# Attention values of two steps made together in every odd step, from three buffers of turned probabilities

## The chip, the cores and the metric

The kernel runs on one core of a Trainium2 chip. The metric is the device time of one execution in microseconds (us); lower is better. The kernel before takes 1966.2 us (median of 3 runs, 1966.16 to 1966.59).

## The reference

The program is a decoder trunk of two layers over 1024 tokens and 1024 columns. The first layer mixes tokens by pooling, the second by attention; each layer also has a SwiGLU block and an update gated by an embedding. The change lies in the attention of the second layer: 16 query heads share 4 key/value heads (4 queries to one), each of 64 columns, and each block of 128 queries sees its own 128 keys and the 128 before.

```
scores = q . k * HEAD_DIM ** -0.5          # a block of 128 queries against 256 keys
scores = where(valid, scores, NEG_INF)     # causal, window of 128
probs  = softmax(concat([scores, sink]))[..., :-1]
out    = probs . v                         # 128 queries x 64 columns for each head
m      = out @ w_o
h      = h + rms_norm(m, mix_post_g)
```

## The kernel before

Attention is worked off in 32 steps. Step n holds one block of 128 queries (t = n // 4) and one key/value head (g = n % 4) with its four query heads. Every engine runs its own list of instructions in order, written out by hand; the lists are tied by semaphores. For step n there are these pieces, named by one letter in the prediction where they are TensorE's:

- S(n), `scores`, L1635: four products of queries and keys on TensorE, into one of two pairs of banks (n odd or even). Before S(n) writes its pair, TensorE waits until the exponentials of step n-2, which read the same pair, are done (`at_probs`).
- `softmax_max`, L1646 and L1651, on VectorE: mask and row maximum of four heads, then the gap to the sink.
- `softmax_exp`, L1660 and L1663, on ScalarE: one small and four large exponentials, from the bank into `probs`, each with its row sum.
- `softmax_recip`, L1671 and L1673, on VectorE, and `softmax_norm`, L1681, on GpSimd: the probabilities are divided by their sums.
- T(n), `turn_probs`, L1689: eight 128x128 transposes on TensorE into banks 4 and 5. It waits for the normed probabilities and until bank 4 and bank 5 of step n-1 have been copied out.
- `probs_copy_even` (VectorE, L1696, bank 4) and `probs_copy_odd` (ScalarE, L1702, bank 5): the turned probabilities are copied to one of two buffers, `pt[n % 2]` (the trace names them tmp and pt). The copy waits for the values of step n-2.
- V(n), `values`, L1716: four products with the values on TensorE, each with 64 output columns, into bank 6 or 7. They wait for both copies of step n and for the output copy of step n-2.
- `att_out`, L1726, on ScalarE: the outputs of step n are copied from the bank to `qo`.

The order of the lists in step n of the loop over 32 steps is:

- TensorE: T(n), S(n+4), V(n-1)
- ScalarE: exponentials of n+2, output copy of n-2, bank 5 copy of n
- VectorE: reciprocal of n+1, maximum of n+3, bank 4 copy of n
- GpSimd: norm of n; behind step 16 and step 18 also the two halves of the first output block (L1753, L1757)

In the last steps TensorE's list holds the first two of the eight blocks of the output projection too (`o_pe_first`, L315 to L317), between S and T of step 31, with pieces of their weights cut on ScalarE (L287) and VectorE (L291). Ahead of the attention ScalarE waits until the query weights are cut, and then issues the load of the row of gains of the next block (`gain_row("ffn1", ...)`, L604). Behind the attention it waits for V(31), issues the load of another row (`post_gain`, L604 too) and cuts the five remaining weight blocks of the output projection; the projection's third block and those behind it wait for these.

Of the kernel before, what the change touches and what calls it, by code (L numbers as in the profile page):

```python
# [22 lines left out]
P = 128  # L23
F32 = mybir.dt.float32
# [3 lines left out]
ACT = mybir.ActivationFunctionType  # L28
AX = mybir.AxisListType

D = 1024
# [3 lines left out]
KD = D // P  # L35
HALF = 512
# [54 lines left out]
def trunk(nc, I, out):  # L91
    ctx = ExitStack()
    with ctx:
# [36 lines left out]
        def region(name, elements, *uses):  # L130

            views = {}
            for use in uses:
                with ExitStack() as inner:
                    for n, shape, dt in use:
                        views[n] = inner.enter_context(nc.sbuf_tensor(n, shape, dt))
            sb(name, [P, elements])
            return views
# [17 lines left out]

        PIECES = [P, 4, 4, P]
        FORM = [P, 4, P]
        GAIN_VIEWS = region("gain_or_late_activations", D, [("gain", [P, D], F32)], [("act_late", [P, 2, HALF], F32)])
        gain, ACT_LATE = GAIN_VIEWS["gain"], GAIN_VIEWS["act_late"]  # L160
        Z = region("Z", 186 * KIB,

# [57 lines left out]
        xn, tmp = [Z["xn0"], Z["xn1"]], Z["tmp"]  # L220
# [19 lines left out]
        ps = ctx.enter_context(nc.psum_tensor("ps", [P, 8, HALF], F32))  # L240
# [17 lines left out]
        BASE, n = {}, 0  # L258
# [7 lines left out]
        w_ready = sem("weights_ready")  # L266
# [335 lines left out]
        def row_load(eng, dst, src, s):  # L602

            eng.dma_start(dst[:, :], src.partition_broadcast(P)).then_inc(s, 16)  # L604
# [66 lines left out]
        m7, up0_last, act_late = Z["m7"], Z["up0_last"], ACT_LATE  # L671
# [942 lines left out]

        STEPS_A = TILES * KV_HEADS
        probs = [DD[f"probs{g}"] for g in range(KV_HEADS)]
        pt = [tmp[:, :].rearrange("p (k c) -> p k c", k=KD), E["pt1"]]
        mask = B["mask"]
        neg_sinks_set = sem("neg_sinks_set")
        at_scores, at_neg_max, at_gap = [sem(f"att_{x}") for x in ("scores", "neg_max", "sink_gap")]  # L1620
# [70 lines left out]

        def probs_copy_even(dve, n):
            dve.wait_ge(at_turned, n + 1)
            if n >= 2:
                dve.wait_ge(at_pv, n - 1)
            dve.tensor_copy(pt[n % 2][:, 0:4, :].rearrange("p a b -> p (a b)"), ps[:, 4, :]).then_inc(at_pt_even, 1)  # L1696

        def probs_copy_odd(act, n):
            act.wait_ge(at_turned, n + 1)
            if n >= 2:  # L1700
                act.wait_ge(at_pv, n - 1)
            act.activation(pt[n % 2][:, 4:8, :].rearrange("p a b -> p (a b)"), ps[:, 5, :], ACT.Copy).then_inc(at_pt_odd, 1)  # L1702

        def values(pe, n):

            t, g = n // 4, n % 4
            pe.wait_ge(at_pt_even, n + 1)
            pe.wait_ge(at_pt_odd, n + 1)
            if n == 0:
                pe.wait_ge(q_copied, 1 + TILES)  # L1710
            if n >= 2:
                pe.wait_ge(at_out, n - 1)
            by_block = pt[n % 2].rearrange("p (m b) c -> p m b c", b=2)
            for b in range(2):
                for r in range(2):
                    last = pe.matmul(ps[HEAD * r:HEAD * (r + 1), 6 + g % 2, (g // 2) * 256:(g // 2 + 1) * 256  # L1716
                                        ].rearrange("p (m c) -> p m c", m=2),
                                     V[:, t + b, g * HEAD:(g + 1) * HEAD], by_block[:, 2 * r:2 * r + 2, b, :],
                                     start=(b == 0), stop=(b == 1))
            last.then_inc(at_pv, 1)  # L1720

        def att_out(act, n):

            t, g = n // 4, n % 4
            act.wait_ge(at_pv, n + 1)
            act.activation(qo[:, t, g * 256:(g + 1) * 256], ps[:, 6 + g % 2, (g // 2) * 256:(g // 2 + 1) * 256], ACT.Copy  # L1726
                           ).then_inc(at_out, 1)
# [282 lines left out]
        def _(act):  # L2010
            def gain_row(name, src):
                row_load(act, gain, src, gain_loaded)
# [125 lines left out]


            staggered(act, q_parts, before=kv_parts, head=False, tail=False)  # L2140
            act.wait_ge(w_ready, BASE["q"] + KD)
            gain_row("ffn1", I["ffn_pre_g"][1])

            def o_cut_hi(k):
                cut_hi(act, BASE["o"], k, w_o[0][:, k, :])
# [7 lines left out]
            for n in range(STEPS_A):  # L2153
                if n + 2 < STEPS_A:
                    softmax_exp(act, n + 2)
                if n == STEPS_A - 1:
                    o_cut_hi(EARLY)
                if n >= 2:
                    att_out(act, n - 2)
                probs_copy_odd(act, n)  # L2160
            for n in range(STEPS_A - 2, STEPS_A):
                att_out(act, n)

            def o_cuts(i, p):
# [3 lines left out]
            def o_gain(i, p):  # L2168
                act.wait_ge(at_pv, STEPS_A)
                row_load(act, post_gain, I["mix_post_g"][1], post_gain_loaded)  # L2170

            staggered(act, [(0, at_first(o_gain)), (0, at_first(o_cuts)), (1, not_first(lambda i, p: o_hi(act, i, p))),
                            (-2, lambda i, p: fn_raw(act, 1, i, p)), (-1, lambda i, p: fn_squares(act, 1, i, p)),
# [184 lines left out]
        @block.tensor  # L2358
        def _(pe):
            pe.wait_ge(first_consts_loaded, 16)  # L2360


            def pool_products(i, p):
                s = s_pool
                pe.wait_ge(s["lo"][p], s.done("lo", i))
                pe.wait_ge(s["added"][p], s.free("added", i))
                pe.wait_ge(pool_w_ready, 2)
                for g in range(len(WINDOWS)):
                    for k in range(2):
                        last = product(pe, banks(2 + 2 * p)[:, g * GROUP:(g + 1) * GROUP],  # L2370
                                       [x[p][:, 2 * g + k, :] for x in (xt_hi, xt_lo)],
                                       [x[:, 2 * g + k, :] for x in w_pool], k == 0, k == 1)
                last.then_inc(s["used"][p], 1)

            staggered(pe, [(1, lambda i, p: pool_band(pe, i, p)), (0, at_last(pool_products)),
                           (-2, lambda i, p: fn_turn(pe, 0, i, p)), (0, not_last(pool_products))],
                      tail=False, unrolled=True)

            def ffn(L):
                last = GROUPS - 1  # L2380
                ffn_pe_first(pe, L)
                ffn_pe_tile(pe, L, 0, 1)
                with pe.Fori(1, last) as g:
                    for t in range(2):
                        ffn_pe_tile(pe, L, g, t)
                for t in range(2):
                    ffn_pe_tile(pe, L, last, t)
                ffn_pe_down(pe, L, last, 0, (last, 1))
                ffn_pe_down(pe, L, last, 1, (last, 1),
                            lambda name, j: turn(pe, S[f"ple{L}"], 0, 0) if (name, j) == ("S1", 1) else None)  # L2390
                keep_busy(pe, 10, 2)
                pe.wait_ge(F["summed"], SUMMED * (half_of(L, GROUPS, 0) + 1))

            def turned(s):
                return lambda i, p: turn(pe, s, i, p)

            ffn(0)
            ple_parts = [[(0, lambda i, p, L=L: ple_pe(pe, L, i, p))] for L in range(2)]
            kv_parts = [(1, turned(s_kv)), (0, lambda i, p: kv_pe(pe, i, p)), (-1, lambda i, p: kv_turn(pe, i, p))]
            def first_scores(i, p):  # L2400
                pe.wait_ge(s_kv["lo"][1], s_kv.done("lo", PAIRS - 1))
                scores(pe, 0)

            q_parts = [(0, at_last(first_scores)), (0, lambda i, p: q_pe(pe, i, p, [0])),
                       (-1, lambda i, p: q_turn(pe, i, p)), (0, at_last(lambda i, p: scores(pe, 1))),
                       (0, lambda i, p: q_pe(pe, i, p, [1]))]
            staggered(pe, ple_parts[0], after=kv_parts, head=False, unrolled=True)
            pe.wait_ge(w_ready, BASE["kv"] + 4)
            staggered(pe, kv_parts, after=q_parts, head=False, tail=False)
            staggered(pe, q_parts, before=kv_parts, head=False, tail=False)  # L2410


            pe.wait_ge(v_copied, TILES)
            scores(pe, 2)
            q_turn(pe, PAIRS - 1, 1)
            scores(pe, 3)
            for n in range(STEPS_A):
                if n == STEPS_A - 1:
                    o_pe_first(pe, range(EARLY))
                turn_probs(pe, n)  # L2420
                if n + 4 < STEPS_A:
                    scores(pe, n + 4)
                if n >= 1:
                    values(pe, n - 1)
            values(pe, STEPS_A - 1)


            staggered(pe, [(0, lambda i, p: o_pe(pe, i, p))], head=False, tail=False, unrolled=True)
            ffn(1)
            staggered(pe, ple_parts[1], head=False, unrolled=True)  # L2430
# [26 lines left out]
```

## Time and profile before

| | |
|---|---|
| runs, median (lowest to highest) | 1966.2 us (1966.16 to 1966.59) |
| the profiled execution | 1965.92 us |
| its span, first to last instruction | 1964.1 us |
| mean granted TensorE clock | 0.998 of full |
| TensorE busy, matmul | 1917.4 us (98%) |
| VectorE busy | 1402.6 us (71%) |
| ScalarE busy | 905.4 us (46%) |
| GpSimd busy | 457.5 us (23%) |
| T of step 0 starts, last V starts | 1000.6 us, 1100.7 us |

Busy time is the union of an engine's instructions; matmuls are pipelined, so that a busy TensorE is not one at its peak. The attention steps are some 5% of the span, and only they are changed. A row of the timeline gives the start, how long the group lasted, the engine, the line, what is written and read, how many instructions the group has, and in brackets how long the engine was idle ahead of it and who ended that. The weight loads of TensorE have the name PEld, instructions that only its or another engine's queue handles a q (ACTq). The engines of the trace are PE (TensorE), DVE (VectorE), ACT (ScalarE) and POOL (GpSimd).

### The profile page before, as it was taken

What the parts mean: (1) busy time and instruction counts of PE and PEld (TensorE: products, weight loads), DVE (VectorE), ACT (ScalarE), POOL (GpSimd) and SP (SyncE); (2) the same over time, 40 slices, a digit from 0 to 9 for tenths busy, and PEclk for the clock granted to TensorE, in tenths of its full rate; (3) what the DMA queues carried; (4) which work ended last, traced back from release to release, by engine and by line L of the source; (5) the groups of instructions that cost most, each with busy time, mean ns of one, the idle gap of its engine ahead of it and who ended that gap; (6) DMA issues with size and microseconds to landing.
All of it is one profiled execution on the core that took longest, in us unless ns stands there. A gap on an engine that the chain in (4) does not pass through costs nothing.

```text
span 1964.1 us, 28703 instructions
## 1 busy us (share of the span) xinstructions
PE 1917.4 (98%) x9198; PEld 1573.6 (80%) x9198; DVE 1402.6 (71%) x2382; ACT 905.4 (46%) x1734; POOL 457.5 (23%) x448
## 2 busy tenths in 40 slices
PE   7899999999999999999999999999999999999998
PEld 7778888888888878888866787788888888888787
DVE  5987777777777786565389658777777777777863
ACT  6744444444444453341178545444444444444531
POOL 2312222222222221010046211212122221222310
PEclk9999999999999999999999999999999999999999
DMA  5333332233333350254200213233333223335201
GB/s 201 108 97 104 91 91 87 76 102 91 107 91 91 92 200 22 78 219 172 86 12 2 66 42 123 71 107 92 98 94 91 86 75 106 91 106 176 99 30 67
DMA packets 222055, 188.50 MB, mean 96 GB/s; under 512 B 12192, under 2 KB 199968, under 8 KB 221984
## 3 DMA queue, kind: packets, MB, share of 16 engines
q1 hardware_dynamic: 217712, 183.38, 29.2%
q10 hardware_dynamic: 4272, 4.21, 0.7%
q8 instruction: 40, 0.66, 0.1%
q14 instruction: 31, 0.25, 0.0%
HBM read 166.58 MB, written 20.97 MB: 95 GB/s over the span
## 4 chain that ended last, share of the span: by engine, by line
PE 89%; DVE 6%; issue 2%; ACT 1%; DMA 1%; POOL 1%; SPq 0%; DVEq 0%; ACTq 0%; POOLq 0%
PE ps L827 14%; PE ps L829 14%; PE ps L828 14%; PE ps L315 7%; PE ps L317 7%; PE ps L316 7%; PE ps L925 7%; PE ps L926 7%; PE ps L924 7%; PE ps L1635 2%; PE ps L1716 1%; PE ps L1689 1%; PE ps L389 1%; PE ps L632 1%; DVE t_lo L1261 1%
## 5 line engine op out<-in xcount | busy, mean ns | idle before, releaser
L1249 DVE TENSOR_TENSOR H<-H,ps 128x512 f32<-128x512 f32 x496 | 328.0, 686 | 112.5 <-PE ps L926 111.7
L1111 POOL TENSOR_TENSOR s_raw<-s_raw,a_raw 128x512 f32<-128x512 f32 x66 | 87.5, 1327 | 766.4 <-DVE s_lo L1162 651.0
L827 PE MATMUL ps<-t_hi,s_hi 128*128 128x512 f32 x528 | 206.4, 391 | 8.1 <-DVE t_lo L1261 5.1
L828 PE MATMUL ps<-t_lo,s_hi 128*128 128x512 f32 x528 | 205.5, 389 | 0.0
L829 PE MATMUL ps<-t_hi,s_lo 128*128 128x512 f32 x528 | 205.5, 389 | 0.0
L1000 ACT ACTIVATE m<-ps 128x512 f32<-128x512 f32 x44 | 26.4, 600 | 265.7 <-PE ps L829 263.3
L827 PE MATMUL ps<-b_hi,a_hi 128*128 128x512 f32 x352 | 137.4, 390 | 0.0
L828 PE MATMUL ps<-b_lo,a_hi 128*128 128x512 f32 x352 | 137.3, 390 | 0.0
L829 PE MATMUL ps<-b_hi,a_lo 128*128 128x512 f32 x352 | 137.2, 390 | 0.0
L924 PE MATMUL ps<-wd_hi,d_ab_hi 128*128 128x512 f32 x336 | 130.7, 389 | 0.0
L925 PE MATMUL ps<-wd_lo,d_ab_hi 128*128 128x512 f32 x336 | 130.7, 389 | 0.0
L926 PE MATMUL ps<-wd_hi,d_ab_lo 128*128 128x512 f32 x336 | 130.7, 389 | 0.0
L827 PEld LDWEIGHTS ps<-t_hi,s_hi 128*128 128x128 f32 x528 | 99.1, 188 | 31.4 <-DVE t_lo L1261 6.8
L829 PEld LDWEIGHTS ps<-t_hi,s_lo 128*128 128x128 f32 x528 | 99.1, 188 | 20.8
L828 PEld LDWEIGHTS ps<-t_lo,s_hi 128*128 128x128 f32 x528 | 99.1, 188 | 20.4
L978 ACT ACTIVATE s_hi<-s_raw 128x512 fp32r<-128x512 f32 x132 | 82.8, 627 | 53.9 <-DVE s_raw L1111 53.9
L1162 POOL TENSOR_TENSOR a_lo<-a_raw,a_hi 128x512 fp32r<-128x512 f32 x60 | 80.8, 1347 | 114.2 <-ACT a_hi L978 114.2
L315 PE MATMUL ps<-w_ple_gate_hi,xt_hi 128*128 128x512 f32 x256 | 101.5, 397 | 1.8 <-DVE w_ple_gate_lo L291 0.8
L317 PE MATMUL ps<-w_ple_gate_hi,xt_lo 128*128 128x512 f32 x256 | 99.9, 390 | 0.0
L316 PE MATMUL ps<-w_ple_gate_lo,xt_hi 128*128 128x512 f32 x256 | 99.7, 389 | 0.0
L941 ACT ACTIVATE ps<-ps 128x512 f32<-128x512 f32 x88 | 51.2, 582 | 97.6 <-PE ps L926 90.8
L1681 POOL TENSOR_TENSOR probs<-probs,recip 128x1024 f32<-128x1024 f32 x32 | 60.6, 1893 | 147.8 <-DVE recip L1673 147.8
(293 smaller groups left out, 5022.8 us busy)
## 6 DMA issues: line engine op xcount, KB each, us to landing
a_raw<-in_w_ff_gate SPq DMA_DIRECT2D x88, 256.0 KB, 2.9
a_raw<-in_w_ff_up SPq DMA_DIRECT2D x88, 256.0 KB, 3.0
s_raw<-in_w_ff_up SPq DMA_DIRECT2D x88, 256.0 KB, 2.9
s_raw<-in_w_ff_gate SPq DMA_DIRECT2D x88, 256.0 KB, 3.1
wd_raw<-in_w_ff_down SPq DMA_DIRECT2D x44, 512.0 KB, 4.3
residual_spill<-H SPq DMA_DIRECT2D x16, 512.0 KB, 2.6
raw<-in_w_ple_gate SPq DMA_DIRECT2D x16, 512.0 KB, 6.0
back<-residual_spill SPq DMA_DIRECT2D x16, 512.0 KB, 5.8
```

The lines of the kernel that those rows point to most:

```text
L315: pe.matmul(out_, lhs[0], rhs[0], start=first, stop=False)
L316: pe.matmul(out_, lhs[0], rhs[1], start=False, stop=False)
L317: return pe.matmul(out_, lhs[1], rhs[0], start=False, stop=last)
L827: pe.matmul(ps[:, bank, :], w[0], x[0], start=fresh and k == 0, stop=False, skip_group_check=not fresh)
L828: pe.matmul(ps[:, bank, :], w[0], x[1], start=False, stop=False, skip_group_check=not fresh)
L829: last = pe.matmul(ps[:, bank, :], w[1], x[0], start=False, stop=k == 3, skip_group_check=not fresh)
L924: pe.matmul(ps[:, bank, :], a[0], wd_hi[:, b, :], start=fresh, stop=False, skip_group_check=not fresh)
L925: pe.matmul(ps[:, bank, :], a[0], wd_lo[:, b, :], start=False, stop=False, skip_group_check=not fresh)
L926: pe.matmul(ps[:, bank, :], a[1], wd_hi[:, b, :], start=False, stop=True, skip_group_check=not fresh).then_inc(F["down"], 1)
L978: act.activation(W[name][0][:, :, :], form_raw(name), ACT.Copy).then_inc(F["form_hi"], 1)
L1111: eng.tensor_tensor(form_raw(name), W_RAW[name][:, :, :], form_raw(other) if other != "A21" else W_RAW["A21"][:, :, :], op).then_inc(summe ...
L1249: dve.tensor_tensor(dst, dst, src, ALU.add).then_inc(F["summed"], 1)
```

## The change

The values of steps n-2 and n-1 are made one after the other in odd steps only; in even steps TensorE makes none. ScalarE copies two outputs in every even step. A third buffer of turned probabilities, laid over the row of gains, replaces the rotation of two by one of three. The load of that row, and the wait ahead of it, leave their place ahead of the attention; the load now stands behind the load of `post_gain`, after the attention.

```
-        GAIN_VIEWS = region("gain_or_late_activations", D, [("gain", [P, D], F32)], [("act_late", [P, 2, HALF], F32)])
+        GAIN_VIEWS = region("gain_or_late_activations", D, [("gain", [P, D], F32)], [("act_late", [P, 2, HALF], F32)],
+                            [("pt2", [P, KD, P], F32)])
-        pt = [tmp[:, :].rearrange("p (k c) -> p k c", k=KD), E["pt1"]]
+        pt = [tmp[:, :].rearrange("p (k c) -> p k c", k=KD), E["pt1"], GAIN_VIEWS["pt2"]]
         def probs_copy_even(dve, n):
             dve.wait_ge(at_turned, n + 1)
-            if n >= 2:
-                dve.wait_ge(at_pv, n - 1)
-            dve.tensor_copy(pt[n % 2][:, 0:4, :].rearrange("p a b -> p (a b)"), ps[:, 4, :]).then_inc(at_pt_even, 1)
+            if n >= 3:
+                dve.wait_ge(at_pv, n - 2)
+            dve.tensor_copy(pt[n % 3][:, 0:4, :].rearrange("p a b -> p (a b)"), ps[:, 4, :]).then_inc(at_pt_even, 1)
         (probs_copy_odd on ScalarE likewise; values reads pt[n % 3])
@@ ScalarE @@
-            act.wait_ge(w_ready, BASE["q"] + KD)
-            gain_row("ffn1", I["ffn_pre_g"][1])
-                if n >= 2:
-                    att_out(act, n - 2)
+                if n % 2 == 0:
+                    for earlier in range(max(n - 3, 0), n - 1):
+                        att_out(act, earlier)
                 probs_copy_odd(act, n)
-            for n in range(STEPS_A - 2, STEPS_A):
+            for n in range(STEPS_A - 3, STEPS_A):
                 att_out(act, n)
             def o_gain(i, p):
                 act.wait_ge(at_pv, STEPS_A)
                 row_load(act, post_gain, I["mix_post_g"][1], post_gain_loaded)
+                gain_row("ffn1", I["ffn_pre_g"][1])
@@ TensorE @@
                 turn_probs(pe, n)
                 if n + 4 < STEPS_A:
                     scores(pe, n + 4)
-                if n >= 1:
-                    values(pe, n - 1)
+                if n % 2 == 1:
+                    for earlier in range(max(n - 2, 0), n):
+                        values(pe, earlier)
             values(pe, STEPS_A - 1)
```

## Rows read from the trace of the kernel before

**Rows 1.** The page's part 4: the chain that ended last, by engine.

```profile
PE 89%; DVE 6%; issue 2%; ACT 1%; DMA 1%; POOL 1%; SPq 0%; DVEq 0%; ACTq 0%; POOLq 0%
```

**Rows 2.** Timeline, TensorE: T of step 2 and T of step 28.

```profile
1007.09 1.09 PE L1689 MATMUL ps<-ident,probs 128*128 128x128 f32 x8
...
1088.16 1.09 PE L1689 MATMUL ps<-ident,probs 128*128 128x128 f32 x8
```

**Rows 3.** Timeline of one step (1041.2 to 1045.4 us), all engines.

```profile
1041.21 1.09 PE L1689 MATMUL ps<-ident,probs 128*128 128x128 f32 x8
...
1042.23 1.14 PE L1635 MATMUL ps<-kT,qo 64*128 64x256 f32 x8
1042.34 0.60 ACT L1702 ACTIVATE pt<-ps 128x512 f32<-128x512 f32 x1 [0.31 <-PE ps L1689]
1042.34 0.69 DVE L1696 COPY pt<-ps 128x512 f32<-128x512 f32 x1
1042.83 0.20 ACT L1660 ACTIVATE sink_exp<-small 128x4 f32<-128x4 f32 x1
...
1043.30 1.08 PE L1716 MATMUL ps<-tmp,V 128*64 128x256 f32 x8
...
1043.39 1.89 POOL L1681 TENSOR_TENSOR probs<-probs,recip 128x1024 f32<-128x1024 f32 x1 [1.21 <-DVE recip L1673]
...
1044.31 1.09 PE L1689 MATMUL ps<-ident,probs 128*128 128x128 f32 x8
...
1044.64 0.22 ACT L1663 ACTIVATION_READ_ACCUMULATOR probs<-ps,small 128x1 f32 x1
1044.73 0.40 ACT L1726 ACTIVATE qo<-ps 128x256 f32<-128x256 f32 x1
...
1045.22 0.16 DVE L1651 TENSOR_TENSOR small<-sinks_placed,small 128x4 f32<-128x4 f32 x1
...
1045.34 1.13 PE L1635 MATMUL ps<-kT,qo 64*128 64x256 f32 x8
```

**Rows 4.** Timeline: the one late step, and S waiting for the exponentials in it.

```profile
1054.55 2.36 POOL L1757 TENSOR_TENSOR o_first_lo<-qo,o_first_hi 128x1024 fp32r<-128x1024 f32 x1
...
1055.36 1.58 DVE L1671 TENSOR_TENSOR sums_placed<-sums,sink_exp 128x4 f32<-128x4 f32 x1
...
1060.99 0.21 ACT L1663 ACTIVATION_READ_ACCUMULATOR probs<-ps,small 128x1 f32 x1
...
1061.26 1.13 PE L1635 MATMUL ps<-kT,qo 64*128 64x256 f32 x8 [0.31 <-ACT probs L1663]
```

**Rows 5.** Timeline, the last steps and the start of the output projection.

```profile
1092.29 0.85 PEld L1689 LDWEIGHTS ps<-ident,probs 128*128 128x128 f32 x8 [0.44 <-POOL probs L1681]
...
1094.11 2.54 DVE L291 TENSOR_TENSOR w_o_lo<-raw,w_o_hi 128x1024 fp32r<-128x1024 f32 x1
...
1096.71 0.19 PEld L315 LDWEIGHTS ps<-w_o_hi,o_first_hi 128*128 128x128 f32 x1 [1.16 <-DVE w_o_lo L291]
...
1099.17 1.08 PE L1716 MATMUL ps<-tmp,V 128*64 128x256 f32 x8
...
1100.08 1.03 PE L1716 MATMUL ps<-pt,V 128*64 128x256 f32 x8
...
1101.17 0.35 ACTq L604 DMA_DIRECT2D post_gain<-in_mix_post_g  x1
...
1101.56 4.86 ACT L287 ACTIVATE w_o_hi<-raw 128x1024 fp32r<-128x1024 f32 x5
...
1103.94 0.50 PE L315 MATMUL ps<-w_o_hi,o_first_hi 128*128 128x512 f32 x1 [1.12 <-DVE w_o_lo L291]
```

**Rows 6.** Timeline: two loads of rows one behind the other, near the start.

```profile
15.29 0.45 ACTq L604 DMA_DIRECT2D gain<-in_ffn_pre_g  x1
```

**Rows 7.** Timeline: the gain load of before, ScalarE's next wait, the first use.

```profile
989.22 0.35 ACTq L604 DMA_DIRECT2D gain<-in_ffn_pre_g  x1
...
993.64 0.20 ACT L1660 ACTIVATE sink_exp<-small 128x4 f32<-128x4 f32 x1 [3.40 <-DVE small L1651]
...
1119.05 1.29 DVE L507 SCALAR_TENSOR_TENSOR tmp<-H,small,gain 128x1024 f32<-128x1024 f32 x1 [2.18 <-POOL small L501]
```

More of the change, by code:

```diff
@@ L1693, in probs_copy_even @@
             dve.wait_ge(at_turned, n + 1)
-            if n >= 2:
-                dve.wait_ge(at_pv, n - 1)
-            dve.tensor_copy(pt[n % 2][:, 0:4, :].rearrange("p a b -> p (a b)"), ps[:, 4, :]).then_inc(at_pt_even, 1)
+            if n >= 3:
+                dve.wait_ge(at_pv, n - 2)
+            dve.tensor_copy(pt[n % 3][:, 0:4, :].rearrange("p a b -> p (a b)"), ps[:, 4, :]).then_inc(at_pt_even, 1)
         def probs_copy_odd(act, n):
             act.wait_ge(at_turned, n + 1)
-            if n >= 2:
-                act.wait_ge(at_pv, n - 1)
-            act.activation(pt[n % 2][:, 4:8, :].rearrange("p a b -> p (a b)"), ps[:, 5, :], ACT.Copy).then_inc(at_pt_odd, 1)
+            if n >= 3:
+                act.wait_ge(at_pv, n - 2)
+            act.activation(pt[n % 3][:, 4:8, :].rearrange("p a b -> p (a b)"), ps[:, 5, :], ACT.Copy).then_inc(at_pt_odd, 1)
         def values(pe, n):
@@ L1712, in values @@
                 pe.wait_ge(at_out, n - 1)
-            by_block = pt[n % 2].rearrange("p (m b) c -> p m b c", b=2)
+            by_block = pt[n % 3].rearrange("p (m b) c -> p m b c", b=2)
             for b in range(2):
@@ L2157, in _ @@
                     o_cut_hi(EARLY)
-                if n >= 2:
-                    att_out(act, n - 2)
+                if n % 2 == 0:
+                    for earlier in range(max(n - 3, 0), n - 1):
+                        att_out(act, earlier)
                 probs_copy_odd(act, n)
-            for n in range(STEPS_A - 2, STEPS_A):
+            for n in range(STEPS_A - 3, STEPS_A):
                 att_out(act, n)
```

## The prediction

> **What bounds the kernel now.** I read the page's chain first: TensorE holds 89% of it [rows 1], so what counts is whether TensorE's list gets shorter or is held up. Then the timeline of the attention, since only its 32 steps are changed. From T(2) at 1007.09 to T(28) at 1088.16 are 26 steps in 81.07 us [rows 2], 3.12 us a step. A single step, T to T, is 44.31 - 41.21 = 3.10 us [rows 3]; the rest of the 81.07, 0.4 us, comes in one late step (below).
>
> In a step TensorE starts T at 1041.21, S at 1042.23, V at 1043.30 and the next T at 1044.31: 1.02 + 1.07 + 1.01 us with no wait for another engine in it [rows 3]. So TensorE sets the pace, but the others stand close behind. VectorE's copy starts at 1042.34 and its last operation of the round ends at 1045.22 + 0.16: 3.04 us of the 3.10. ScalarE copies at 1042.34, has its four exponentials done at 1044.64 + 0.22 = 1044.86, and S starts at 1045.34 [rows 3]. That S is the one which needs these exponentials (they read the banks that it overwrites), so it has 0.48 us to spare. This spare time is what the change draws on.
>
> **The change part by part.**
>
> *Two values in one go.* The list per two steps goes from T S V T S V to T S T S V V. What is saved is a change between kinds of products. V(30) and V(31) stand directly behind one another in the last steps: 1100.08 - 1099.17 = 0.91 us [rows 5], against 1.01 from V to T. V(31) even had a true wait there, so 0.91 is no lower than a smooth passage. The second V then costs 0.85 for its own eight instructions plus the 0.10 that V to T has above 0.91: 0.95. A pair is 0.91 + 0.95 = 1.86 instead of 2.02. No row shows S to T; I take it as 1.07, like S to V. TensorE alone would then need 1.02 + 1.07 + 1.02 + 1.07 + 1.86 = 6.04 us for two steps, 0.16 less than 6.20. The bounds for V to V are 0.85 (nothing at the boundary) and 1.01 (as much as from V to T).
>
> *The score wait.* Take an even step a, T(a) starting at 0. Its end lets ScalarE copy bank 5 at 1042.34 - 1041.21 = 1.13. Behind this copy in ScalarE's list stand the exponentials of a+3, done 1044.86 - 1042.34 = 2.52 later, at 3.65 [rows 3]. S(a+5), in the odd step, may start only then. The step from the last exponential to the S that waited for it is 1061.26 - (1060.99 + 0.21) = 0.06 [rows 4], so S(a+5) starts at 3.71 at the earliest. In the old order TensorE got there at 4.12 (T S V T before it). In the new one, T(a) S(a+4) T(a+1), it is there at 1.02 + 1.07 + 1.02 = 3.11, and waits 0.60 us. Nothing of ScalarE's list can move forward, since the copy ahead of the exponentials needs T(a). Behind the waiting S stand V(a-1), V(a) and T(a+2), so all of them are late:
>
> 3.71 + 1.07 (S to V) + 1.86 (two V) = 6.64 us from T(a) to T(a+2), 0.44 more than 6.20.
>
> T(a+2) again starts the same circle, so the loss is paid in each pair. It ends where S ends: S(a+5) exists up to 31, so a = 2, 4, ... 26, 13 pairs. 13 x 0.44 = 5.7 us.
>
> *The other lists in this circle.* VectorE's two rounds need 2 x 3.04 = 6.08 of 6.64. After its copy at 1.13 it is ready for the copy of a+1 at 4.17, though T(a+1) ends at 3.2; that copy is done by 4.9, and T(a+2) asks for it at 6.64. T(a+1) needs the copy of a, done at 1.13 + 0.69 = 1.82, and comes at 2.09: covered by S(a+4). GpSimd's norm takes 1.89 [rows 3] and is ready two us or more ahead of its T. ScalarE's second output copy (0.40) waits for V(a), done at 6.7, and lies ahead of the copy that waits for T(a+2) at 7.8. The third buffer and the looser wait cost nothing: the copies keep their size, and what they waited for was long done.
>
> *The late step.* At 1054.55 GpSimd has 2.36 us of extra work, VectorE's small operation is held for 1.58 [rows 4], and TensorE loses the 0.4 us named above. In the new order VectorE has more room, 0.56 a pair, but the hold also meets exponentials that now bound: its round in question ends 8.8 us after T(16) instead of the 8.3 at which ScalarE asks for it, so about 0.5 us are lost again. I count no difference.
>
> *The gain row.* The load ahead of the attention is issued at 989.22, and ScalarE's next exponential starts only at 993.64, held by VectorE for 3.40 us [rows 7]. So neither the 0.35 us of issue nor the wait ahead of it is worth anything there: 0. Behind the attention the issue stands on the path: post_gain's is issued at 1101.17 for 0.35 us, and the first cut follows at 1101.56 [rows 5]. The second issue goes between. Such a second one took 0.45 at 15.29 [rows 6]; I take 0.40 (0.35 to 0.45). Its data is asked for at 1119.05 [rows 7], some 16 us after the issue, by a queue with nothing else but post_gain ahead: hidden.
>
> *The last steps.* From T(28) to T(31) nothing should move. T(29) is held by the copy of step 28 as before, within 0.1 us. T(30) comes 0.7 us later, with V(27) and V(28) ahead of it, but V(29) leaves the place behind it, and block 1 of the projection still waits for the weight cut of 1094.11 to 1096.65 [rows 5], whose length GpSimd's norm sets. Behind T(31) there are now three V and not two: V(31) starts 0.91 later. From the end of V(31) runs a chain without slack: output copy, issue of the loads, cut at 1101.56, its second half, and TensorE at 1103.94, idle for 1.12 us before [rows 5]. So TensorE restarts later by 0.91 + 0.40 = 1.3 us, and behind it nothing on the page waits longer than TensorE itself.
>
> *Sum.* 5.7 + 1.3 + 0 = +7.0 us. The profiled execution took 1965.92, of which 1964.1 is span and 1.8 lies around it and stays: 1972.9. The runs' median stands 0.3 above the profiled one, so 1973.2 us.
>
> **Rivals.**
>
> *The saving without the wait.* If S found its exponentials done, by 0.60 us a pair earlier than I read, TensorE alone would give 13 x -0.16 = -2.1, and with the end's +1.3 it is -0.8: 1965.4 us, no slower than before. It decides from exponentials done before 3.11 after T(a). For it speaks that TensorE waits for no one in the steady step; against it the order of ScalarE's list, and that S did wait for ScalarE in the late step [rows 4].
>
> By the Trainium skill, TensorEngine Tiling (Array Packing), section Key Properties, changing the tiling mode drains the engine, while changing only the tile doesn't. S uses half the rows, V half the columns, T all: six such changes per two steps become five. This rule speaks for the rival's gain, and rows 5 against rows 3 agree with it (0.91 from V to V, 1.01 from V to T); it doesn't touch the wait.
>
> *Full boundaries and late copies.* If V to V costs 1.01, and each other passage of the circle is at its upper end (S to V 1.07, V to T 1.01, wait to S 0.1 instead of 0.06), two steps take 1.13 + 2.52 + 0.10 + 1.07 + 2.02 = 6.84, 0.64 more. 13 x 0.64 = 8.3, and with 1.4 at the end +9.7: 1975.9 us. For it: the waits between V and V are three. Against it: the 0.91 of rows 5.
>
> *The end is hidden.* If the restart at 1103.94 is covered otherwise, only 5.7 remain: 1971.9. Against it stands the idle time of 1.12 us that rows 5 show.
>
> **How the numbers follow.** The forecast with the hidden end has 0.79 (of it 0.07 for the latter), full boundaries 0.08, the saving without the wait 0.13. What can be told from no change is 0.2%, 3.9 us. The first two are slower by more than that: 0.87. The third is within it, but for 0.03 in which the passages save 0.4 us a pair: same 0.10, faster 0.03. The low end with V to V at 0.85 and 0.9 at the end is 13 x 0.38 + 0.9 = +5.8, 1972.0; I reach further down, to 1969.8, for stalls of half the size that part of the rival would leave, and up to 1976.0 for the full boundaries.
>
> **What would show it.** In the profile after: T(a) to T(a+2) 6.6 us, S of odd steps idle before for about 0.6 us and released by ScalarE's exponentials (L1663), in 13 places; S of even steps without wait; V to V 0.9; T(2) to T(28) 86.8 us; three V behind T(31); two issues ahead of the first cut and the projection's restart 1.3 us later after T(31). It would be wrong if odd steps' S starts without a wait, or if VectorE's copy of the odd steps holds T(a+2).

## The result

The changed kernel takes 1975.1 us (median of 5 runs, 1973.92 to 1975.63) against 1966.2 (5 runs, 1965.17 to 1967.18): 8.9 us slower, ratio 1.0043 with a 95% interval of 1.0032 to 1.0054. The forecast was 1973.2, in a range from 1969.8 to 1976.0. The profiled execution took 1974.01 us, near the low end of its runs, with a span of 1972.2, 8.1 us more than before.

The page's chain of the changed kernel (by engine, share of the span) has 3% of ScalarE where there was 1% [rows 1]:

```profile
PE 88%; DVE 6%; ACT 3%; issue 2%; POOL 1%; DMA 1%; POOLq 0%; ACTq 0%; DVEq 0%
```

Where these 3% lie is seen in the chain in order of time (start, length, what), here from T of an even step to the next:

```profile
1040.25 1.04 PE ps L1690 x8
...
1042.00 1.42 ACT probs L1664 x7
...
1043.88 1.14 PE ps L1636 x8
1045.01 1.88 PE ps L1717 x16
1046.89 1.04 PE ps L1690 x8
```

The chain now leaves TensorE in each pair of steps: T, then ScalarE with its exponentials, then S and both V. The same stretch in the timeline (lines have moved by one against before) is to be held against rows 3:

```profile
1040.18 1.09 PE L1690 MATMUL ps<-ident,probs 128*128 128x128 f32 x8
...
1041.21 1.13 PE L1636 MATMUL ps<-kT,qo 64*128 64x256 f32 x8
1041.31 0.60 ACT L1703 ACTIVATE tmp<-ps 128x512 f32<-128x512 f32 x1 [0.63 <-PE ps L1690]
...
1042.27 1.09 PE L1690 MATMUL ps<-ident,probs 128*128 128x128 f32 x8
...
1043.61 0.22 ACT L1664 ACTIVATION_READ_ACCUMULATOR probs<-ps,small 128x1 f32 x1
...
1043.88 1.14 PE L1636 MATMUL ps<-kT,qo 64*128 64x256 f32 x8 [0.52 <-ACT probs L1664]
...
1044.94 1.08 PE L1717 MATMUL ps<-pt,V 128*64 128x256 f32 x8
...
1045.86 1.03 PE L1717 MATMUL ps<-tmp,V 128*64 128x256 f32 x8
...
1046.82 1.09 PE L1690 MATMUL ps<-ident,probs 128*128 128x128 f32 x8
```

From T(a) to the next even T are 6.64 us, to the last digit what was walked out. The reader sees each leg: T to the copy 1.13, copy to the last exponential 2.52, S 3.70 after T, S to V 1.06, V to V 0.92, V to T 0.96. S of the even step, at 1041.21, waits for no one. S of the odd step could have followed T(a+1) 1.02 us behind it, at 1043.29, and starts 0.59 later (the prediction has 0.60; the bracket's 0.52 counts from the modelled end of T). The waits of 1010 to 1090 us (waiter, releaser: total us, times, longest) hold 12 of the 13 odd steps; the 13th is S at 1090.77:

```profile
PE ps L1636 <- ACT probs L1664: 5.8, 12, 0.5
```

In the last steps there are three V behind T(31) and two load issues ahead of the first cut; rows 5 showed two and one. The last row, at 1111.03, is where TensorE goes on with the projection behind its wait for a cut; it is called the restart here (1103.94 before):

```profile
1103.76 1.04 PE L1690 MATMUL ps<-ident,probs 128*128 128x128 f32 x8
...
1104.72 1.08 PE L1717 MATMUL ps<-pt,V 128*64 128x256 f32 x8
...
1105.64 1.03 PE L1717 MATMUL ps<-tmp,V 128*64 128x256 f32 x8
...
1106.50 1.03 PE L1717 MATMUL ps<-pt,V 128*64 128x256 f32 x8
...
1107.59 0.35 ACTq L605 DMA_DIRECT2D post_gain<-in_mix_post_g  x1
1107.97 0.64 ACTq L605 DMA_DIRECT2D gain<-in_ffn_pre_g  x1
1108.66 3.90 ACT L288 ACTIVATE w_o_hi<-raw 128x1024 fp32r<-128x1024 f32 x4 [0.70 <-issue]
...
1111.03 0.50 PE L316 MATMUL ps<-w_o_hi,o_first_hi 128*128 128x512 f32 x1 [1.92 <-DVE w_o_lo L292]
```

The 8.1 us of the two spans come together so, each from the same two events in both traces:

| stretch | before | after | difference |
|---|---|---|---|
| start to T(2) | 1007.09 | 1006.94 | -0.15 |
| T(2) to T(28), at 1088.16 and 1093.71 | 81.07 | 86.77 | +5.70 |
| T(28) to T(31) | 10.04 | 10.05 | 0 |
| T(31) to the projection's restart | 5.74 | 7.27 | +1.53 |
| restart to the first row of ScalarE's L1000 (L1001 after) behind it | 120.42 | 121.19 | +0.77 |
| from there to the end | 739.7 | 740.0 | +0.2 |

The fifth line had no term in the forecast. Part of it is TensorE's granted clock. A row of the windows gives busy time of each engine, then the clock (1.00 is 2.4 GHz, 0.50 would be 1.2 GHz), DMA share and GB/s; after:

```profile
1208.70:1214.30 5.60, 5.53 (x33) 5.41 (x34) 4.81 (x7) 2.00 (x4) 1.27 (x1) 0.70 1.02 363
```

and the same place before:

```profile
1201.50:1208.00 6.50, 5.18 (x38) 4.75 (x39) 6.16 (x8) 2.82 (x6) 1.26 (x1) 1.00 0.96 340
```

TensorE was granted 0.70 on average over 5.6 us in one execution (0.50 from 1209 to 1212) and full speed in the other. TensorE's rows at this place, before and then after, tell what that cost:

```profile
1201.55 1.09 PE L518 MATMUL ps<-ident,tmp 128*128 128x128 f32 x8 [2.17 <-DVE tmp L507]
...
1206.59 0.50 PE L827 MATMUL ps<-t_hi,s_hi 128*128 128x512 f32 x1 [1.26 <-DVE t_lo L1261]
```

```profile
1208.77 1.85 PE L519 MATMUL ps<-ident,tmp 128*128 128x128 f32 x8 [2.10 <-DVE tmp L508]
...
1214.13 0.50 PE L828 MATMUL ps<-t_hi,s_hi 128*128 128x512 f32 x1
```

The changed kernel is 7.22 us behind at the first pair of rows and 7.54 at the second. Most of the time that the low clock took lies where TensorE would else have waited 1.26 us for VectorE, so 0.32 us are left of it. Another 0.13 gather ahead of this place, and the last 0.32 of the line behind it, where VectorE stands idle before L1163, which it doesn't in the kernel before:

```profile
1229.43 0.69 DVE L1163 TENSOR_TENSOR s_lo<-s_raw,s_hi 128x512 fp32r<-128x512 f32 x1 [0.46 <-DVE a_raw L1112]
```

ScalarE's first L1001 then waits 1.53 us for VectorE instead of 1.18. The seven other versions with three buffers (below) have 1.53 or 1.54 too; the kernel before and its three versions, as well as two_buffers, have 1.17 or 1.18. So it comes with the change; why isn't shown.

The low clock isn't tied to the change. Kernels without any pairing (exp1_before and mixed_before, below) had it at this place too, and the profiled execution of the kernel before had it at 81 us (0.83 over 80 to 90 us), where that of the changed kernel hadn't.

### The profile page after: what moved, and what is told of

It is laid out like the page before. It is cut to its first block, busy times and chain, and to the rows that moved or that the text cites. A ratio compares the mean times of both kernels' runs of the same rounds, so it can differ in the third digit from the quotient of the medians.

```text
span 1972.2 us, 28701 instructions
## 1 busy us (share of the span) xinstructions
PE 1916.8 (97%) x9198; PEld 1576.2 (80%) x9198; DVE 1401.9 (71%) x2382; ACT 906.7 (46%) x1734; POOL 457.7 (23%) x448
## 4 chain that ended last, share of the span: by engine, by line
PE 88%; DVE 6%; ACT 3%; issue 2%; POOL 1%; DMA 1%; POOLq 0%; ACTq 0%; DVEq 0%
PE ps L828 14%; PE ps L830 13%; PE ps L829 13%; PE ps L316 7%; PE ps L318 7%; PE ps L317 7%; PE ps L925 7%; PE ps L927 7%; PE ps L926 7%; PE ps L1717 1%; ACT probs L1664 1%; PE ps L1636 1%; PE ps L390 1%; PE ps L633 1%; PE ps L1690 1%
## 5 line engine op out<-in xcount | busy, mean ns | idle before, releaser
L1001 ACT ACTIVATE m<-ps 128x512 f32<-128x512 f32 x44 | 26.4, 600 | 265.5 <-PE ps L830 262.8
L1163 POOL TENSOR_TENSOR a_lo<-a_raw,a_hi 128x512 fp32r<-128x512 f32 x60 | 80.9, 1348 | 114.4 <-ACT a_hi L979 114.4
```

## Experiments

**One part undone: values in every step.**

```
-                if n % 2 == 1:
-                    for earlier in range(max(n - 2, 0), n):
-                        values(pe, earlier)
+                if n >= 1:
+                    values(pe, n - 1)
```

> The changed kernel with one part undone: TensorE makes the values of step n-1 in every step, as before; third buffer, paired output copies and the late gain load stay. Theory (the pairing takes 1.01 us from between T(a) and S(a+5), and S then waits for the exponentials): the wait is gone, T(2) to T(28) is 81.1 us again and not 86.8, and only the second load issue in front of the weight cuts stays (0.64 us in the trace after): about 1966.9 us. Rival (the third buffer, the paired output copies or the moved load cost the time): it stays at 1971 us or more.

Measured: 1968.8 us, ratio to before 1.0014 (1.0004 to 1.0023). The pace is back: T(4) and T(6), below, are 6.20 us apart, and T(28) at 1087.57 is 81.07 after T(2) at 1006.50.

```profile
1012.71 1.09 PE L1690 MATMUL ps<-ident,probs 128*128 128x128 f32 x8
...
1018.91 1.09 PE L1690 MATMUL ps<-ident,probs 128*128 128x128 f32 x8
```

So the third buffer and the paired output copies cost nothing in the steps, and the 5.7 us are the pairing's. The total missed the expected 1966.9 by 1.9. The profiled execution shows three things that the expectation lacked. The second load issue took 0.94 us here and not 0.64. VectorE's pause before L1163 is there too, 0.3. And TensorE had stood idle for 2.20 us at the restart, at 1104.56, behind which the clock was low (windows); it is 0.62 us behind the kernel before there, and 2.21 at 1140 us:

```profile
1102.00:1104.50 2.50, 0.36 (x2) 0.00 (x0) 1.22 (x2) 2.30 (x3) 0.00 (x0) 1.00 0.89 344
1104.50:1109.00 4.50, 4.44 (x12) 3.51 (x13) 4.50 (x6) 3.49 (x4) 0.00 (x0) 0.62 0.09 34
1109.00:1113.00 4.00, 4.00 (x19) 3.28 (x18) 1.19 (x2) 0.00 (x0) 0.00 (x0) 1.00 0.00 0
```

From 1106.16 to 1108.72 matmuls started 0.43 us apart, and 0.23 before and behind this stretch: at half clock. The 0.62 is the mean of a window that also holds some time at full clock. By the Trainium skill, TensorE: Matmul & The Clock Gate, section What's actually happening, the engine's clock has just these two speeds and is lowered when it has been idle; the trace agrees with the two speeds (0.43 against 0.23).

**A shorter ScalarE in the circle.** ScalarE makes one exponential over 1024 columns instead of four over 256, in the changed kernel and in the one before (exp1), and two over 512 in the changed one (exp2). What these kernels leave out is the maximum and the sum of each head: the heads of a group share those of the first, so their outputs are not the reference's. The cut is shown for one exponential; `2` stands for `4` with two:

```
-            for m in range(GQA):
-                sl = slice(m * 256, (m + 1) * 256)
+            for m in range(0, GQA, 4):
+                sl = slice(m * 256, (m + 4) * 256)
                 last = act.activation(probs[g][:, sl], banks(2 * par)[:, sl], ACT.Exp, ...
```

> The changed kernel with two exponentials over 512 columns a step instead of four over 256, biased by one head's maximum and with one sum for two heads each. ScalarE's part of the circle shrinks by about 0.5 us. Theory: T(a) to T(a+2) shrinks by as much, from 6.64 to 6.15 us, still a little above the 6.05 at which TensorE alone runs it (one exponential a step gave 6.05), and S of the odd step still waits for a trace of time, about 0.1 us. Rival (a fixed cost of the pairing, which a shorter ScalarE only hides when it is short enough): it stays at 6.64 or falls at once to 6.05.

> The changed kernel, but with one exponential over 1024 columns a step instead of four over 256, biased by the first head's maximum and with one sum for all four heads; everything else is issued as it was. ScalarE's part in the circle shrinks from 1.92 to about 1.2 us. Theory: the circle would take 5.9 us for two steps, so that it no longer bounds; TensorE's own 6.04 or VectorE's 6.08 do: T(a) to T(a+2) about 6.1 us, no S waits for the exponentials, about 1967.5 us. Rival (the pair of values itself or TensorE's boundaries cost the 0.44 us): T(a) to T(a+2) stays at 6.64 and the time at 1974 to 1975 us.

> The same single exponential in the kernel before. Theory: there the exponentials had 0.48 us to spare and bound nothing in the steady steps: T(a) to T(a+2) stays at 6.20 us; only the first steps, where ScalarE was late, get up to 2 us shorter: 1964 to 1966 us. Against exp1_after it then shows what the pairing is worth by itself: 0.1 to 0.16 us for two steps. Rival (ScalarE was a bound of the kernel before too): T(a) to T(a+2) falls below 6.1.

Measured: exp2_after 1967.7 us in one run; exp1_after 1967.0, ratio 1.0003 (0.9993 to 1.0013); exp1_before 1964.5, ratio 0.9993 (0.9983 to 1.0002). T(4) and T(6) of exp2_after, 6.15 us:

```profile
1013.52 1.09 PE L1692 MATMUL ps<-ident,probs 128*128 128x128 f32 x8
...
1019.67 1.09 PE L1692 MATMUL ps<-ident,probs 128*128 128x128 f32 x8
```

and of exp1_after, 6.05 us, with the one wait of TensorE for another engine between T(4) and T(28):

```profile
1012.95 1.09 PE L1692 MATMUL ps<-ident,probs 128*128 128x128 f32 x8
...
1019.00 1.09 PE L1692 MATMUL ps<-ident,probs 128*128 128x128 f32 x8
...
1058.66 1.06 PE L1692 MATMUL ps<-ident,probs 128*128 128x128 f32 x8 [1.18 <-DVE tmp L1699]
```

The pair shrinks with ScalarE's part as far as TensorE's own 6.05 (4 exponentials 6.64, 2: 6.15, 1: 6.05), while in the kernel before one exponential leaves it at 6.20 (T at 1012.05 and 1018.25). This is the score wait, and nothing fixed in the pairing. The kernels with one exponential also give what the pairing is worth alone: 0.15 us saved per pair. Even that isn't banked: T(2) to T(28) takes 80.46 us in exp1_after and 80.69 in exp1_before, 0.23 less and not 13 x 0.15 = 2.0. At the late step VectorE, held by GpSimd, made TensorE wait 1.18 us, and T(2) to T(4) took 6.61, since T(3) waited 0.52 for VectorE's copy. With the last steps and what follows, exp1_after is 2.5 us behind exp1_before.

**The paired output copies undone, values still paired.**

```
-                if n % 2 == 0:
-                    for earlier in range(max(n - 3, 0), n - 1):
-                        att_out(act, earlier)
+                if n >= 2:
+                    att_out(act, n - 2)
                 probs_copy_odd(act, n)
-            for n in range(STEPS_A - 3, STEPS_A):
+            for n in range(STEPS_A - 2, STEPS_A):
                 att_out(act, n)
```

> The changed kernel, but with ScalarE copying the output of step n-2 in every step, as before. In odd steps ScalarE then waits for V(a-1) ahead of its copy of bank 5 of step a+1, and the exponentials of a+4 are behind that. Theory: by the same walk through the lists S waits in even steps too, and T(a) to T(a+2) is 7.8 us: 13 x 1.18 = 15 us more than the changed kernel, about 1990 us. Rival (ScalarE's order matters little, since its spare time takes it up): within 2 us of 1975.

Measured: 1987.7 us, ratio 1.0107 (1.0090 to 1.0124). T stands at 1028.65 and 1036.36, 7.71 us for two steps (7.8 expected), and S waits in both:

```profile
1030.83 1.13 PE L1636 MATMUL ps<-kT,qo 64*128 64x256 f32 x8 [1.09 <-ACT probs L1664]
...
1033.42 1.13 PE L1636 MATMUL ps<-kT,qo 64*128 64x256 f32 x8 [0.43 <-ACT probs L1664]
...
1035.61 0.39 ACT L1727 ACTIVATE qo<-ps 128x256 f32<-128x256 f32 x1 [2.25 <-PE ps L1717]
```

The last row is the cause: ScalarE stands still 2.25 us in front of an output copy whose V isn't made yet, with the exponentials of the next score behind it.

**Two buffers instead of three** (the copies wait `at_pv >= n - 1` again and use `pt[n % 2]`).

> The changed kernel with two buffers of turned probabilities instead of three, each copy waiting for the values of two steps before as in the kernel before. The copies of the odd step a+1 then wait for V(a-1), which stands behind S(a+5). Theory: as in out_single, ScalarE's copy of step a+1 comes 2.4 us later, the exponentials of a+4 too, and S waits in even steps as well: T(a) to T(a+2) about 7.9 us, near 1990 us. Rival (the third buffer is not needed, as the copies have time enough): 6.64 us as in the changed kernel, 1975 us.

Measured: 1990.1 us in one run. T at 1036.94 and 1044.71: 7.77 us; S waits for the exponentials in even and odd steps, 0.65 to 0.74 each. With these lists the third buffer is thus a condition of the pairing.

**S behind the pair of values in odd steps.**

```
+                if n % 2 == 1:
+                    for earlier in range(max(n - 2, 0), n):
+                        values(pe, earlier)
                 if n + 4 < STEPS_A:
                     scores(pe, n + 4)
```

> The changed kernel with S(a+5) behind the two V of the odd step instead of ahead of them: T(a+1) V(a-1) V(a) S(a+5). S then comes 1.9 us later than TensorE could, so the exponentials of a+3 are long done and the circle of the changed kernel is open. Theory (all lists are bound to one another, and VectorE has 0.06 us a step to spare): now VectorE's maximum of a+5 starts late, its copy of step a+2 too, and T(a+3) waits for this copy (DVE, L1697), about 0.7 us in each pair; T(a) to T(a+2) about 6.8 us, 1977 us. Rival (the score wait was all that stood against the pairing): 6.05 us for two steps, 1967.5 us.

Measured: 1976.9 us in one run. No S waits for exponentials, and VectorE's copy holds T of the odd step instead; 6.77 us from T(a) to T(a+2):

```profile
1034.06 1.09 PE L1690 MATMUL ps<-ident,probs 128*128 128x128 f32 x8
...
1036.89 1.06 PE L1690 MATMUL ps<-ident,probs 128*128 128x128 f32 x8 [0.67 <-DVE pt L1697]
...
1040.83 1.09 PE L1690 MATMUL ps<-ident,probs 128*128 128x128 f32 x8
```

Giving the score wait what it wants breaks VectorE's list. The first rival's gain isn't to be had by this order either.

**The restart of the projection.** In gain_behind the changed kernel's gain load stands behind the five cuts. In early_before and early_after, ScalarE cuts blocks 3 and 4 together with block 2, ahead of its last copies, and VectorE the second halves of blocks 2 and 3 ahead of its last copy (the later cuts start that much further on):

```
                 if n == STEPS_A - 1:
-                    o_cut_hi(EARLY)
+                    for k in range(EARLY, EARLY + 3):
+                        o_cut_hi(k)
...
+                if n == STEPS_A - 1:
+                    o_cut_lo(2)
+                    o_cut_lo(3)
                 probs_copy_even(dve, n)
```

> The changed kernel with the moved load of the gain row issued behind the five weight cuts instead of ahead of them. Theory (ScalarE's first cut waits for both issues): the first cut starts at the end of the output copy and of post_gain's issue, the restart is 0.6 to 0.7 us earlier after T(31): 1974.4 us. The row is still needed only 8 us after the projection's first tile, so no wait on it. Rival (the issue runs beside ScalarE's work): restart 7.27 us after T(31) as in the changed kernel.

> The kernel before with three weight blocks of the output projection cut earlier: ScalarE cuts blocks 2, 3 and 4 where it cut block 2 alone (ahead of its last copy of turned probabilities, where it was idle for 4 us), and VectorE cuts the second halves of blocks 2 and 3 ahead of its last copy. Theory (the projection's restart in the last steps is on the path, so that what delays it counts in full): the idle 1.12 us before block 3 is gone, 1.4 us less: 1964.8 us. Rival (the restart is hidden by what follows): no change, 1966.2.

> The same earlier cuts in the changed kernel. Theory: the restart no longer waits for the two load issues and the cut behind them, 2.1 us less (block 3 stood idle 1.92 us): 1973.0 us; the 5.7 us of the 13 pairs stay, so it remains slower than the kernel before by 6.5 to 7. Rival (part of the 8.9 us comes from elsewhere than pairs and restart): the distance to early_before stays near 8.

Measured: gain_behind 1973.6 us, with T(31) at 1103.74 and the restart at 1110.33, 6.59 us and not 7.27: the second issue's 0.68 are shown. Its trace has that issue at 1108.10, beside the first cut, though it stands behind all five in the list. The median is 1.5 us below the changed kernel's and 0.8 below the expected 1974.4; what the other 0.8 are isn't shown. early_before 1965.0 us, ratio 0.9995 (0.9986 to 1.0004), early_after 1971.6, ratio 1.0028 (1.0017 to 1.0038). In early_before and early_after TensorE's wait for block 3 is gone, and they stand 6.6 us apart, within the 6.5 to 7 expected. early_after gained 3.5 us where 2.1 were expected. The mean granted clock of its eight runs is 0.9993, that of the changed kernel's five 0.9984, so part of the rest is likely the low clock; that wasn't tried by itself.

**A version that beats both.** early_before, with T(31) ahead of block 1 and VectorE's cuts 2 and 3 behind its last copy:

```
                 if n == STEPS_A - 1:
-                    o_pe_first(pe, range(EARLY))
+                    o_pe_first(pe, range(1))
                 turn_probs(pe, n)
+                if n == STEPS_A - 1:
+                    o_pe_first(pe, range(1, EARLY))
```

> A version to beat both, from what the runs showed of the last steps: the kernel before (values in every step), with the weight blocks 2 to 4 cut early on ScalarE, blocks 2 and 3 cut on VectorE right behind its last copy, and T(31) ahead of block 1 of the projection instead of behind it, so that block 1 fills the time in which T(31) is copied. Theory: besides the 1.4 us of early_before another 1.1 us, since V(30) and V(31) no longer stand behind block 1, its weight cut and the wait for the copies: 1963.8 us. Rival (VectorE's cut of block 1, held by GpSimd's norm of step 31, is late for the copy too): no more than early_before's 1965.0.

Measured: 1963.8 us, ratio 0.9989 (0.9980 to 0.9998), 2.4 us faster than before: a small gain, just clear of none.

```profile
1095.93 1.03 PE L1689 MATMUL ps<-ident,probs 128*128 128x128 f32 x8
...
1096.82 0.50 PE L315 MATMUL ps<-w_o_hi,o_first_hi 128*128 128x512 f32 x1
...
1099.32 1.03 PE L1716 MATMUL ps<-pt,V 128*64 128x256 f32 x8
...
1100.29 0.50 PE L315 MATMUL ps<-w_o_hi,o_first_hi 128*128 128x512 f32 x1
```

T(28) is at 1088.27, so V(31) starts 11.05 us behind it instead of 11.92 (1100.08, as rows 5 have it, and not the 1100.7 of the table of the time before), and block 2 follows without a gap.

## Why the prediction was right

- *The score wait* was the main term, and all of it holds: 3.70 us from T(a) to S(a+5) against 3.71, 6.64 for two steps against 6.64, 5.70 us over the 13 pairs against 5.7. v_single takes it away by the order, exp2_after and exp1_after by a shorter ScalarE, with TensorE's order kept.
- *Two values in one go*: V to V 0.92 (0.91 taken), TensorE alone 6.05 a pair (6.04 taken). The rival in which this saving stands alone is refuted; and exp1_after shows that most of the saving would go to VectorE's copies even then, which I hadn't priced in that rival.
- *The Trainium skill's rule on tiling modes* (TensorEngine Tiling (Array Packing), Key Properties) agreed with V to V against V to T, and with the 0.15 us a pair between exp1_after and exp1_before, where one change of mode of six is gone. That the drain is what the 0.15 us are isn't shown.
- *The late step*: T(16) at 1053.46 to T(20) took 13.7 us, 0.4 more than two pairs, as before: no difference, as counted.
- *The gain row*: nothing ahead of the attention and no wait for its data, right. The second issue was mis-sized: 0.40 taken, from 0.45 in rows 6, and 0.64 measured. In the other versions it took 0.45 (exp1_after, exp2_after, s_last), 0.77, 0.80, 0.91 and 0.94. The one row of before was the shortest of its kind, and I took still less.
- *The last steps*: T(28) to T(31) unchanged, right (10.04 and 10.05). V(31) 0.86 later (0.91 taken). The restart is 1.53 later and not 1.3.
- *The sum* of what was counted is 5.70 + 1.53 = 7.2 us against 7.0. The medians lie 8.9 apart, so 1.7 us had no term. Of them 0.3 are the low clock at 1209 us, 0.3 VectorE's pause before L1163, and 0.2 to 0.3 small shifts elsewhere. The last 0.8 lie between the profiled pair and the medians, within the 1.7 us over which the runs of the changed kernel spread. That the change makes the low clock more frequent isn't shown: the runs' mean granted clock is 0.9984 for its five, and 0.9985 for the 59 of the kernel before that were taken beside the experiments.
- *The rival of full boundaries* gave 1975.9, nearer to the measured time than the forecast, but not by its mechanism: V to V is 0.92. The range reached up to 1976.0 for this rival alone. That the measured 1975.1 lies in it is thus partly luck: the mechanism was right, and the 1.7 us that nobody counted fell into room left for something else.

## What to carry to other kernels

When work is taken out from between two instructions of the fastest list, see whose result the second one needs, and how late that is: here 0.48 us of spare time stood against 1.01 us taken away. Grouping work on one engine makes its pace uneven, and the lists that hang on it by a single buffer see only the shortest interval, not the mean. An engine that is busy for 3.04 us of a 3.10 us round is a bound too, and a gain on another one is worth at most what it leaves.

## What the runs showed of the hardware

A load's issue on ScalarE's queue took 0.34 to 0.35 us when it came first, and 0.45 to 0.94 us as the second one right behind another. In the changed kernel the first cut behind the two issues waited for them (idle 0.70 us with "issue" as its reason). In gain_behind, with the cuts ahead of it in the list, the issue ran beside them.

TensorE's granted clock fell to half for some microseconds behind idle gaps of 2.20 us in v_single, 2.03 in out_single (0.67 over 5 us), 2.10 in the changed kernel at 1209 us, and 1.81 in two_buffers at 1110 us. It didn't fall behind those of 1.12 and 1.92 at the restart of the kernel before and the changed one, nor behind 2.06 in two_buffers at 1128 us and 2.17 in the kernel before at 1201 us. So the length of the gap alone doesn't tell. In v_single the fall cost TensorE 1.6 us (0.62 to 2.21 above); at 1209 us, where a wait for VectorE lay behind it, 0.3.

VectorE's small operation on two operands outside the banks, started beside a 2.36 us operation of GpSimd, lasted until that one ended: 1.58 us instead of 0.15 [rows 4], and 1.73 in the changed kernel. A weight cut beside GpSimd's norm took 2.54 instead of 1.22 [rows 5].
